# Stick-breaking attention's entry: the last gate tile divided among the first heads' scores, value blocks in another order, sums of later blocks without copies

## The reference, cut to what matters

```python
logits = einsum("bhtd,bhsd->bhts", q, kb) * Dh ** -0.5
log_keep = where(mask, log_sigmoid(-logits), 0.0)
after = sum(log_keep, -1, keepdims=True) - cumsum(log_keep, -1)
wts = where(mask, exp(log_sigmoid(logits) + after), 0.0)
o = einsum("bhts,bhsd->bhtd", wts, vb)
...
o = o * silu(z)          # z: the gate, half of h @ w_in
return o @ w_out
```

## Time and profile before

| | |
|---|---|
| time, median of 3 runs | 1233.19 us (1231.24 to 1233.85) |
| the profiled execution: time, span | 1230.61 us, 1228.7 us |
| mean granted PE clock | 0.990 of full speed |
| busy, share of the span | PE 96%, PEld 74%, ACT 44%, DVE 40%, POOL 30% |
| the last block ahead of the heads ends on PE | 636.7 us |
| the heads end on PE | 752.0 us |
| DMA | 121.14 MB, mean 99 GB/s |

### The profile page before, as it was taken

One profiled execution on the slowest core, in us unless ns is written; L12 is line 12 of the kernel. 1 busy time (PEld: TensorE's weight loads), 2 busy tenths in 40 slices (PEclk: granted clock), 3 DMA queues, 4 the chain that ended last, 5 costly groups with the idle time before them and its releaser, 6 DMA issues.

```text
span 1228.7 us, 21193 instructions
## 1 busy us (share of the span) xinstructions
PE 1176.3 (96%) x8874; PEld 914.7 (74%) x8874; DVE 487.4 (40%) x919; ACT 538.8 (44%) x924; POOL 370.7 (30%) x148
## 2 busy tenths in 40 slices
PE   5999999999989999999999999999999999999998
PEld 3788886677668888777765666888887777777767
DVE  4575544544324472341314553640202332231462
ACT  4232237633336343543547774333125433754430
POOL 0143343132265314344331001332144122333250
PEclk8999999999999999999999999999999999999999
DMA  9723331356650232322422100323132321324201
GB/s 318 231 69 102 102 101 37 103 188 223 208 180 2 69 103 70 102 81 91 129 69 73 26 14 1 124 89 103 34 106 84 111 78 35 103 70 155 87 1 69
DMA packets 105761, 121.14 MB, mean 99 GB/s; under 512 B 5145, under 2 KB 91705, under 8 KB 105673
## 3 DMA queue, kind: packets, MB, share of 16 engines
q1 hardware_dynamic: 101424, 116.14, 29.9%
q10 hardware_dynamic: 4248, 3.73, 1.1%
HBM read 111.47 MB, written 2.10 MB: 92 GB/s over the span
## 4 chain that ended last, share of the span: by engine, by line
PE 84%; ACT 6%; DVE 4%; issue 3%; DMA 1%; ACTq 0%; SPq 0%; POOL 0%; DVEq 0%
PE ps L2039 42%; PE ps L2846 4%; PE ps L2644 3%; PE ps L2635 2%; PE ps L2180 2%; PE ps L2085 2%; PE ps L2426 2%; PE ps L2669 2%; PE ps L2648 1%; PE ps L2778 1%; PE ps L2123 1%; PE ps L2203 1%; PE ps L2256 1%; PE ps L2731 1%; PE ps L2453 1%
## 5 line engine op out<-in xcount | busy, mean ns | idle before, releaser
L604 POOL TENSOR_TENSOR wlo<-raw,whi 128x2048 fp32r<-128x2048 f32 x53 | 245.1, 4624 | 586.1 <-ACT whi L768 571.5
L768 ACT ACTIVATE whi<-raw 128x2048 fp32r<-128x2048 f32 x52 | 99.3, 1911 | 203.2 <-PE ps L2039 164.2
L610 POOL TENSOR_TENSOR wlo<-raw,whi 128x2048 fp32r<-128x2048 f32 x10 | 46.4, 4641 | 111.0 <-ACT whi L857 62.7
L1277 ACT ACTIVATE p<-sc,nmx 128x256 f32<-128x256 f32 x64 | 32.0, 501 | 49.6 <-PE ps L2765 29.5
L857 ACT ACTIVATE whi<-raw 128x2048 fp32r<-128x2048 f32 x11 | 21.1, 1918 | 62.7 <-PE ps L2039 62.7
L2039 PE MATMUL ps<-hC_hi,whi 128*128 128x512 f32 x184 | 47.1, 398 | 0.8 <-POOL wlo L604 0.8
L1861 DVE CUSTOM_DVE_ANT_0 sc<-ps,biast 128x256 f32<-128x256 f32 (+1 forms) x64 | 23.1, 394 | 62.2 <-PE ps L2756 33.3
L2039 PE MATMUL ps<-hC_lo,whi 128*128 128x512 f32 x184 | 45.5, 390 | 0.0
L2039 PE MATMUL ps<-hC_hi,wlo 128*128 128x512 f32 x184 | 45.4, 389 | 0.0
L2039 PEld LDWEIGHTS ps<-hC_hi,whi 128*128 128x128 f32 x184 | 33.8, 188 | 14.9 <-issue 6.4
L2039 PEld LDWEIGHTS ps<-hC_lo,whi 128*128 128x128 f32 x184 | 34.5, 188 | 7.4
(11 more groups left out here) (514 smaller groups left out, 2822.5 us busy)
## 6 DMA issues: line engine op xcount, KB each, us to landing
raw<-in_w_in_dram SPq DMA_DIRECT2D x24, 1024.0 KB, 5.2
raw<-in_w_in_a_dram SPq DMA_DIRECT2D x16, 1024.0 KB, 5.8
raw<-in_w_ada_dram SPq DMA_DIRECT2D x8, 1024.0 KB, 5.5
late_w<-in_w_ada_dram SPq DMA_DIRECT2D x8, 1024.0 KB, 5.5
raw<-in_w_kv_dram SPq DMA_DIRECT2D x8, 1024.0 KB, 5.1
raw<-in_w_in_b_dram SPq DMA_DIRECT2D x8, 1024.0 KB, 5.3
ada_a<-in_w_ada_dram SPq DMA_DIRECT2D x4, 1024.0 KB, 10.0
ada_b<-in_w_ada_dram SPq DMA_DIRECT2D x4, 1024.0 KB, 13.2
```

Source lines behind the costliest of these rows:

```text
L604: pool.tensor_tensor(wlo[:, s, :], raw[:, s, :], whi[:, s, :].bitcast(F32), ALU.subtract).then_inc(lo_ready, 1)
L610: pool.tensor_tensor(wlo[:, s, :], raw[:, s, :], whi[:, s, :].bitcast(F32), ALU.subtract).then_inc(lo_ready, 1)
L768: A(whi[:, s, :], raw[:, s, :], ACT.Copy).then_inc(hi_ready, 1)
L1277: A(p2[:, n % 2, 256 * e:256 * e + 256], sc2[:, n % 2, 256 * e:256 * e + 256], ACT.Exp, scale=-1.0, bias=nmx[:, grp, t, 2 * hp + e:2 * hp ...
```

## The change

The last gate tile is no longer made as tile 3 of its block but in PSUM bank 7, by 24 single matmuls in three groups of eight: before `qk(0)`, between `qk(0)` and `qk(1)`, and after `qk(1)`. `qk(1)` no longer waits for its copy; the copy on DVE stands behind the first head's sums, and pair kt = 1, whose value products use bank 7, waits for it. DVE takes the magnitudes of head 1 ahead of head 0's keep logs. ACT's conversion of the second half of D_OUTB's weights moves from `head_exps(1)` to behind `head_weights(1)`. The value blocks are taken as 0 and 3 in odd steps and 1 and 2 in even ones (0, 3, 1, 2 for the last pair). The sums over later blocks lose their two copies: the part that was copied is now read by PE from `att` itself, so `later` has four matmuls for blocks 0 and 1 instead of two, and `after0` and `after1` shrink to 256 and 128 columns (their declarations and a pad are left out below).

```diff
@@ -1179,8 +1179,6 @@
         if n >= 5:
             act.wait_ge(pv_full, (n - 5) // 2 + 1)
         A(later_att(n), later_logits(n), ACT.Abs).then_inc(head_logged, 1)
-        if n == 1:
-            next_hi(D_ZB + 1, 1)
         act.wait_ge(head_logged, 3 * n + 1)
         act.wait_ge(abs_first, n + 1)
         A(att(n), att(n), ACT.Exp, scale=-1.0).then_inc(head_logged, 1)
@@ -1207,6 +1205,8 @@
             head_logs(n)
         if n:
             head_weights(n - 1)
+        if n == 2:
+            next_hi(D_ZB + 1, 1)
         if n >= 5 and n % 2:
             yb_hi((n - 5) // 2)
     act.wait_ge(gate_done, 8)
@@ -1776,15 +1776,19 @@
         dve.wait_ge(yb_done, kt + 1)
         TT(yB_lo[:, kt, :], ybt[:, kt % 2, :], yB_hi[:, kt, :].bitcast(F32), ALU.subtract).then_inc(yblo_done, 1)
 
-    dve.wait_ge(dense_full, 4 * (D_ZB + 2))
-    dve.wait_ge(gate_done, 7)
-    copy(zsT[:, KD - 1, :], dense[3]).then_inc(gate_done, 1)
-    for n in range(HB):
+    def magnitudes(n):
         dve.wait_ge(qk_full, n + 1)
         if n >= 5:
             dve.wait_ge(pv_full, (n - 5) // 2 + 1)
         dve.tensor_scalar(att(n, 0, 512).bitcast(I32), logits(n, 0).bitcast(I32), 0x7FFFFFFF, None,
                           ALU.bitwise_and).then_inc(abs_first, 1)
+
+    magnitudes(0)
+    for n in range(HB):
+        if n == 0:
+            magnitudes(1)
+        elif n >= 2:
+            magnitudes(n)
         if n >= 5 and n % 2:
             yb((n - 5) // 2)
             if n >= 7:
@@ -1797,11 +1801,14 @@
         dve.wait_ge(nlk_done, 2 * n + 2)
         if n:
             dve.wait_ge(sfx_full, n)
-        copy(after1[:, 0:128], k2[:, 0:128])
-        TT(after1[:, 128:256], k2[:, 128:256], k3, ALU.add).then_inc(after_step, 1)
-        copy(after0[:, 0:128], k1[:, 0:128])
+        TT(after1[:, 0:128], k2[:, 128:256], k3, ALU.add).then_inc(after_step, 1)
+        TT(after0[:, 0:128], k1[:, 128:256], k2[:, 0:128], ALU.add)
         dve.wait_ge(after_step, n + 1)
-        TT(after0[:, 128:384], k1[:, 128:384], after1[:, :], ALU.add).then_inc(after_done, 1)
+        TT(after0[:, 128:256], k1[:, 256:384], after1[:, 0:128], ALU.add).then_inc(after_done, 1)
+        if n == 0:
+            dve.wait_ge(dense_full, 4 * (D_ZB + 2))
+            dve.wait_ge(gate_done, 7)
+            copy(zsT[:, KD - 1, :], ps[:, 7, :]).then_inc(gate_done, 1)
     yb(KD - 2)
     yb_low(KD - 3)
     yb_low(KD - 2)
@@ -2611,8 +2618,22 @@
     dense_unit(D_ZB, 0, hB)
     head_sums(SQ_QB + 4, G_QB + 4)
     dense_unit(D_ZB, 1, hB, later_sums(SQ_QB + 4, G_QB + 4))
-    dense_block(D_ZB + 1, hB)
-
+    dense_unit(D_ZB + 1, 0, hB)
+    pe.wait_ge(lo_ready, 2 * (D_ZB + 1) + 2)
+    bank_free(D_ZB + 1, 2)
+    products_ch(D_ZB + 1, 1, 0, hB).then_inc(dense_full, 1)
+
+    def last_gate(qs):
+
+        hi, lo = unit(whi, 1, "ch"), unit(wlo, 1, "ch")
+        for q in qs:
+            which, k = divmod(q, KD)
+            w, x = ((hi, hB_hi), (lo, hB_hi), (hi, hB_lo))[which]
+            last = mm(ps[:, 7, :], w[:, k, 128:256], x[:, k, :], start=q == 0, stop=q == 23)
+            if q == 23:
+                last.then_inc(dense_full, 1)
+
+    last_gate(range(8))
 
     pe.wait_ge(kqn_done, 16)
     pe.wait_ge(bf_ready, 1)
@@ -2621,8 +2642,8 @@
 
         s, kt = n % 2, n // 2
         rs, other = slice(64 * s, 64 * s + 64), slice(64 - 64 * s, 128 - 64 * s)
-        if n < 2:
-            pe.wait_ge(gate_done, 7 + n)
+        if n == 0:
+            pe.wait_ge(gate_done, 7)
         pe.wait_ge(swapped[kt % 2], 64 * (kt // 2 + 1))
         for j in range(NT):
             if n >= 2 and j < 2:
@@ -2644,18 +2665,21 @@
             return mm(logits(n, j), C("negtri"), att(n, off[j], off[j] + 512 - 128 * j), start=False, stop=True,
                       skip_group_check=True)
 
-        def later(j, total):
-            return mm(logits(n, j, 128), C("negones"), total, start=False, stop=True, skip_group_check=True)
+        def later(j, at, total, width):
+            return mm(logits(n, j, at)[:, 0:width], C("negones"), total, start=False, stop=True,
+                      skip_group_check=True)
 
         pe.wait_ge(nlk_done, 2 * n + 1)
         own(0)
         pe.wait_ge(nlk_done, 2 * n + 2)
         own(1)
         pe.wait_ge(after_done, n + 1)
-        later(0, after0[:, :]).then_inc(sfx_first, 1)
-        later(1, after1[:, :])
+        later(0, 128, att(n, off[1], off[1] + 128), 128)
+        later(0, 256, after0[:, :], 256).then_inc(sfx_first, 1)
+        later(1, 128, att(n, off[2], off[2] + 128), 128)
+        later(1, 256, after1[:, :], 128)
         own(2)
-        later(2, att(n, off[3], off[3] + 128))
+        later(2, 128, att(n, off[3], off[3] + 128), 128)
         own(3).then_inc(sfx_full, 1)
 
     def weighted(kt, blocks):
@@ -2663,13 +2687,15 @@
         pe.wait_ge(wt_done, 4 * kt + 4)
         if kt >= 2:
             pe.wait_ge(yb_done, kt - 1)
+        if kt == 1:
+            pe.wait_ge(gate_done, 8)
         for j in blocks:
             for n in (2 * kt, 2 * kt + 1):
                 rs = slice(64 * (n % 2), 64 * (n % 2) + 64)
                 last = mm(ps[rs, 6 + kt % 2, 128 * j:512], Vb[:, j, 64 * n:64 * n + 64],
                           att(n, off[j], off[j] + 512 - 128 * j), start=j == 0, stop=True,
                           skip_group_check=True)
-        if j == NT - 1:
+        if blocks[-1] == 2:
             last.then_inc(pv_full, 1)
 
     def first_out_b(ks):
@@ -2689,16 +2715,18 @@
                     last.then_inc(dense_full, 1)
 
     qk(0)
+    last_gate(range(8, 16))
     qk(1)
+    last_gate(range(16, 24))
     for n in range(1, HB + 2):
         if n <= HB:
             suffix_sums(n - 1)
         if n == HB + 1:
             first_out_b(range(1))
         if n == HB + 1:
-            weighted(KD - 1, range(NT))
+            weighted(KD - 1, (0, 3, 1, 2))
         elif n >= 3:
-            weighted((n - 3) // 2, range(1) if n % 2 else range(1, NT))
+            weighted((n - 3) // 2, (0, 3) if n % 2 else (1, 2))
         if n + 1 < HB:
             qk(n + 1)
     first_out_b(range(1, KD))
```

More of the change, by code:

```diff
@@ L148, in mixer_stack @@
                 att_a = sb("att_a", [128, 3, 1280], F32, s2)
-                after1 = sb("after1", [128, 256], F32, s2)
+                after1 = sb("after1", [128, 128], F32, s2)
             with ExitStack() as s2:
@@ L212, in mixer_stack @@
             ybt = sb("ybt", [128, 2, 512], F32, B)
-            after0 = sb("after0", [128, 384], F32, B)
-            sb("pad_b", [128, KD * T - 3968], F32, B)
+            after0 = sb("after0", [128, 256], F32, B)
+            sb("pad_b", [128, KD * T - 3840], F32, B)
             with ExitStack() as s2:
```

## The result

The changed kernel takes 1240.31 us (median of 5 runs, 1238.53 to 1242.98) against 1233.19 us; ratio 1.0067, 95% interval [1.0053, 1.0081]. A second measurement gave 1.0057 [1.0036, 1.0078]. So it is slower, by 7 to 8 us where 4.6 were forecast; its profiled execution took 1242.46 us, span 1240.5. All runs compared here are of the same, fast state.

What follows compares the result with a forecast made beforehand. PE was taken as the bound, busy nearly all of the span. +3.9 + 1.8 - 1.2 + 0.1 = +4.6 us gave 1235.2 on the profiled execution, 1237.8 on the median; range 1234.0 to 1240.5.

Steps and rivals of the forecast that it cites:

- Part 1: Entry to the heads: dividing the last gate tile fills PE's 2.40 us wait, making the entry 4.0 us earlier.
- Part 2: Before head 4's scores: swaps queued behind the moved conversion stall PE 7.6 us; scores 4 start 3.9 us later (+3.9).
- Rival A: Head 4's swaps land in time, so the entry's gain stays: faster, 1228.0 us; chance 0.12.
- The clock: After the stall at head 4, PE runs at half rate for 3.4 to 3.6 us: +1.8 us.
- Rival B: After the stall the clock holds at 2.4 GHz or recovers in idle time: +2.8, 1236.0 us; chance 0.18.
- Part 3: Steady heads: value blocks 0 and 3, then 1 and 2, even out the steps to 6.58 us: -1.2 us.
- Rival C: Steady heads: the two engines' equal cycles jostle and steps keep their mean: +5.8, 1239.0 us; chance 0.07.
- Part 4: Later sums without copies, PE's two matmuls split into four: +0.1 us, at most 0.3 for 16 heads.
- The sum: Whole kernel: all terms together make it 4.6 us slower, 1237.8 us on the median; chance 0.60.

Runs made afterwards that it cites:

- swap_first: Changed kernel with SP issuing the swap for heads 4 and 5 ahead of the second half of w_out_b's last load; 1229.97 us, 0.9976.
- only_move: Kernel before with only the conversion of D_OUTB's second half moved behind head 1's weights; 1241.43 us, 1.0093.
- busy_43: Changed kernel with 43 spare dense matmuls on PE ahead of head 4's scores; 1240.05 us.
- pad_heads: Kernel before with 8 spare semaphore instructions for PE in each head, 128 in all; outside the heads 2.3 us slower than before.
- split_pad: Kernel before with only the later sums split, plus 8 spare semaphore instructions for PE in each head; 1.0022.
- busy: Changed kernel with 30 spare dense matmuls on PE ahead of head 4's scores; 1240.24 us.
- conv_back: Changed kernel with the conversion of D_OUTB's second half put back inside head 1's exponentials; 1232.72 us, 1.0003.

## Why the prediction was right and wrong, step by step

- **Part 1**, entry 4.0 us earlier: right; 4.1. The order of PE was as written, the 2.40 us wait went. One detail was off: a wait of 0.54 us ahead of head 3's scores, hidden by the stall.
- **Part 2**, stall of 7.6 us, scores 4 3.9 us later: right; 7.73, and 670.69 - 4.66 = 666.03 for 665.98. swap_first removed all of it and only_move made it alone (+9.5 for 9.7). Rival A's deciding point, the swap not behind the conversion, was the right one: with it the changed kernel is faster than before, by 2.4 us and not by A's 5.2.
- **The clock**, +1.8: right; 2.05 by busy_43 against after, and the slow stretch of work was 4.2 us where 3.4 to 3.6 were taken. Rival B falls. By the Trainium skill, page "TensorE: Matmul & The Clock Gate", section "Part 1: The HAM clock gate", the slow clock is what an idle PE falls back to; the trace agrees, with 0.50 from 668.0 us on, behind 5 us without PE work.
- **Part 3**, -1.2: right; -1.21, -1.22 and -1.29 in three pairs, steps of 6.58 or 6.59. Rival C falls.
- **Part 4**, +0.1 with at most 0.3: wrong, and it is the step that failed. The matmuls cost what was said (1.10 us in a head for 1.08, +0.21 in the heads' stage). The error was to end the sum there: "a loss beyond that would need a weight load that isn't hidden". It costs +3.0 +- 0.7 us alone, almost all of it outside the heads. What the runs show in its place: 128 more PE instructions, spare or of the split, move the transfers of its instructions, one meets a weight load 380 us behind the heads, that load lands 1 to 2 us later, and PE's first products with `vB` wait for what hangs on it (2.3 us outside the heads for the spare instructions of pad_heads). How much of the split's own +3.0 that makes stays open, since split_pad, where this wait is gone, still has +2.3 +- 0.7; so does the cause of the part in the scan.
- **The sum**: heads' stage +4.57 and +4.88 for +4.6; total +7.9 and +6.8. The difference is of the size of Part 4's excess, and it put the time above the forecast, though the sign and the mechanism in the heads held. The range should have had a term for what an edit does to the length of PE's list, beyond its own work.

## What to carry to other kernels

When an instruction moves, follow the engine queues behind it to their last item: here one ACT conversion held a POOL product, a load and, only because they stood behind that load in one queue, the swaps that PE needed; issuing them first turned +7 to +8 us into -2. When PE's instruction count changes, look at fixed later stages as well as at the edited one, and test with spare instructions. An edit that gives the critical path nothing, as the split did, isn't free: with it the improved kernel stood at 0.9976 [0.9964, 0.9989], without it at 0.9955 [0.9939, 0.9971]. And a wait that a profile names "issue" isn't yet a wait for nothing: look in the code for the semaphore, and compare its distance to the DMAs behind it in two kernels.

## What the runs showed of the hardware that was not expected

- With 128 spare PE instructions of no work, a stage 380 us behind the last of them took 16.8 us where it took 14.4 and 14.5 before; with 256 it took 13.1 (12.8 to 14.5 in all profiles without more PE instructions).
- A 1 MB weight load that takes 5.4 us took 6.3 to 7.6 in seven of eight profiles in which a 16 KB transfer of instructions fell within 0.6 us of its issue. Another that takes 5.9 to 6.5 us took 7.9 to 9.2 where one came 2.6 or 2.7 us after it, and the swaps behind it 7.8 us instead of 5.6.
- The clock fell during a wait of only 2.89 us right behind 7.1 us of dense matmuls (busy), and in conv_back at 652 us behind a wait of 1.62 us. Behind the entry's wait of 2.40 us, which nine profiles share, it kept 1.00 in four, both of the kernel before among them, and fell for 3.4 us in five (pad_heads: 0.51 from 645.3 to 648.6 us). So one profile doesn't tell whether a short wait lets the clock fall.
